# Time-step columns widened by a third of the z product, and the delta rule's diagonal blocks packed 64 wide

## What is computed

```
proj = x @ w_in                       # x 256x1024
z, xbc, dt_raw = proj[..., :1024], proj[..., 1024:2560], proj[..., 2560:2576]
xbc = silu(causal_dwconv(xbc, conv_w) + conv_b)
dt = softplus(dt_raw + dt_bias)       # 16 columns
da = dt * (-exp(a_log));  xdt = xs * dt
...                                   # chunk states, cumulative decays, y
y = y * silu(z)
```

## Time and profile before

| | us |
|---|---|
| median of 3 runs | 1343.62 |
| lowest, highest | 1341.12, 1346.0 |
| the profiled execution | 1346.43 |
| its span, first to last instruction | 1344.5 |
| PE busy in the span | 1290.2 |
| POOL busy | 947.8 |
| ACT busy | 648.8 |
| DVE busy | 416.1 |

### The profile page before, as it was taken

How to read it: one execution, slowest core, us unless ns; L and a number is a source line. 1 busy time by engine, 2 the same in 40 slices (tenths; PEclk the granted TensorE clock), 3 DMA queues, 4 the chain that set the end, 5 groups by cost and what they waited for, 6 DMA issues and landing times.

```text
span 1344.5 us, 19614 instructions
## 1 busy us (share of the span) xinstructions
PE 1290.2 (96%) x8203; PEld 1154.0 (86%) x8203; DVE 416.1 (31%) x755; ACT 648.8 (48%) x841; POOL 947.8 (70%) x416
## 2 busy tenths in 40 slices
PE   6999999999999999999999999999988878999997
PEld 6988988878899988897899889998878658999885
DVE  5526325442222210045552131101153452101124
ACT  5673545755455553343444454435356544443442
POOL 6864246846969888756478778879976346786983
PEclk9999999999999999998999999999999998999999
DMA  8744134534656555635355756646637334663651
GB/s 276 210 128 126 48 110 132 182 108 127 220 152 199 183 195 195 188 93 159 104 173 188 245 169 183 175 138 211 224 113 265 108 94 129 172 193 119 234 189 47
DMA packets 117966, 218.60 MB, mean 163 GB/s; under 512 B 9415, under 2 KB 18934, under 8 KB 117750
## 3 DMA queue, kind: packets, MB, share of 16 engines
q1 hardware_dynamic: 113888, 209.92, 50.6%
q10 hardware_dynamic: 3990, 7.42, 1.6%
HBM read 216.27 MB, written 1.05 MB: 162 GB/s over the span
## 4 chain that ended last, share of the span: by engine, by line
PE 89%; DVE 7%; ACT 2%; issue 1%; DMA 1%; ACTq 0%; DVEq 0%
PE acc L1868 13%; PE acc L1870 13%; PE acc L1871 13%; PE acc L1861 12%; PE acc L1863 12%; PE acc L1862 12%; PE pm L1876 8%; PE acc L1819 1%; PE acc L1820 1%; PE acc L1821 1%; ACT pm L548 1%; PE pm L1785 1%; DMA ct<-in_consts 1%; DVE XTlo L1063 0%; DVE pm L1734 0%
## 5 line engine op out<-in xcount | busy, mean ns | idle before, releaser
L533 POOL TENSOR_TENSOR wlo<-raw,whi 128x1024 fp32r<-128x1024 f32 (+2 forms) x412 | 947.6, 2325 | 382.1 <-ACT whi L548 380.6
L548 ACT ACTIVATE whi<-raw 128x1024 fp32r<-128x1024 f32 (+2 forms) x412 | 412.4, 1019 | 354.1 <-PE acc L1871 154.2
L1868 PE MATMUL acc<-XThi,whi 128*128 128x256 f32 x1424 | 406.8, 286 | 5.5 <-issue 2.9
L1870 PE MATMUL acc<-XTlo,whi 128*128 128x256 f32 x1424 | 405.3, 285 | 0.0
L1871 PE MATMUL acc<-XThi,wlo 128*128 128x256 f32 x1424 | 405.3, 285 | 0.0
L1868 PEld LDWEIGHTS acc<-XThi,whi 128*128 128x128 f32 x1424 | 275.8, 194 | 6.9 <-issue 3.7
L1870 PEld LDWEIGHTS acc<-XTlo,whi 128*128 128x128 f32 x1424 | 275.8, 194 | 0.2
L1871 PEld LDWEIGHTS acc<-XThi,wlo 128*128 128x128 f32 x1424 | 275.7, 194 | 0.0
L1861 PE MATMUL acc<-whi,XThi 128*128 128x512 f32 (+3 forms) x320 | 125.8, 393 | 2.6 <-DVE xbcT L1492 1.6
L1863 PE MATMUL acc<-whi,XTlo 128*128 128x512 f32 (+3 forms) x320 | 121.5, 380 | 0.0
L1862 PE MATMUL acc<-wlo,XThi 128*128 128x512 f32 (+3 forms) x320 | 121.5, 380 | 0.0
(11 more groups left out here) (405 smaller groups left out, 1657.7 us busy)
## 6 DMA issues: line engine op xcount, KB each, us to landing
raw<-in_w_in SPq DMA_DIRECT2D x68, 512.0 KB, 3.7
raw<-in_w_ff SPq DMA_DIRECT2D x64, 512.0 KB, 3.7
raw<-in_w_in_mix SPq DMA_DIRECT2D x44, 512.0 KB, 3.6
raw<-in_w_down SPq DMA_DIRECT2D x44, 512.0 KB, 4.3
raw<-in_w_gate SPq DMA_DIRECT2D x40, 512.0 KB, 3.6
raw<-in_w_up SPq DMA_DIRECT2D x40, 512.0 KB, 3.7
raw<-in_w_branch SPq DMA_DIRECT2D x16, 512.0 KB, 3.5
raw<-in_w_out_mix SPq DMA_DIRECT2D x16, 512.0 KB, 3.5
```

The source lines that it names most:

```text
L533: nc.gpsimd.tensor_tensor(wlo[:, u % SPLIT, 0:nk, 0:width], raw[:, u % RAW, 0:nk, 0:width], whi[:, u % SPLIT, 0:nk, 0:width].bitcast(F32), ...
L548: return nc.scalar.activation(out_, in_, func, **k)
L1868: T.matmul(o, wh[:, fs], hi[:, k, :], start=opens and f % 2 == 0, stop=False, skip_group_check=True)
L1870: T.matmul(o, wh[:, fs], lo[:, k, :], start=False, stop=False, skip_group_check=True)
```

## The change

Part A. The 16 columns of dt get the first 336 columns of z beside them, as one chunk "dt" of 352 columns; `pieces` loads them as two transfers. The rest of z is two chunks of 344. The chunk dt moves ahead of xbc2, and the small steps move with it: xs is transposed after one unit of xbc2, the C B step after one unit of mz1, sc0 gives its first unit to cover `rows(2)`, and DVE does dt's softplus before the convolution of xbc2. The z columns of chunk dt stay in `acc` until ACT has taken them, after the softplus, whose scratch lies in the free columns of the same bank.

Part B. The two 64x64 matrices of a tile lie one above the other: matrix j on partitions 64j to 64j+63, all eight tiles side by side in 512 columns in place of 1024. Each 128x128x128 matmul becomes two, one for each j: 64x64 with 64 moving columns on rows and columns 64j of the array for the levels and for the first transposition (now a product with the identity). For keys with keys and queries it is 128 rows by 64 columns; for u 64x64 with 128 moving columns; for w 64 rows by 128 columns with 64 moving columns. ACT's copies and DVE's masks and subtractions of these steps get half as many columns. The step that makes `d_e` is 16 operations on 64 partitions in place of 8 on 128.

```diff
 def pieces(c0, width):
...
+    if width == SSD_H + ZA:
+        return (c0, SSD_H), (0, ZA)
...
     for c in range(3):
+        if c == 2:
+            g.append(("dt", "w_in_mix", KD, M_DT, SSD_H + ZA, "T"))
         g.append((f"xbc{c}", "w_in_mix", KD, M_XBC + c * W, W, "F"))
-    g.append(("dt", "w_in_mix", KD, M_DT, SSD_H, "T"))
     for c in range(2):
-        g.append((f"mz{c}", "w_in_mix", KD, c * W, W, "T"))
+        g.append((f"mz{c}", "w_in_mix", KD, ZA + c * ZB, ZB, "T"))
...
-            high_halves(begun("mz0", 2) + AHEAD)
+            high_halves(begun("xbc2", 2) + AHEAD)
+            act.wait_ge(S["dt_done"], 1)
+            fn(zz[:, :, 0:ZA], accT("dt")[:, :, SSD_H:], ACT.Silu).then_inc(evac_at("dt")[0], 1)
+            high_halves(landed("xbc2") + AHEAD)
+            silu2(2)
+            leave("mz0", zz[:, :, ZA:ZA + ZB], ACT.Silu)
+            logs()
+            high_halves(begun("mz1", 1) + AHEAD)
             act.wait_ge(S["s_bt"], 1)
...
-                    mm(flat(i), kT[:, i:i + P], kT[:, i:i + P])
-                    last = mm(flat(2 * BANK + i), kT[:, i:i + P], qT[:, i:i + P])
+                    for j in range(2):
+                        at, cols = i // 2, slice(i + 64 * j, i + 64 * j + 64)
+                        mm(pm[diag(j), 0, at:at + 64], kT[:, cols], kT[:, cols])
+                        last = mm(pm[diag(j), 1, at:at + 64], kT[:, cols], qT[:, cols])
...
+            def blocks(hf, bank, lhs, rhs):
+
+                for k in range(4):
+                    for j in range(2):
+                        at = slice(hf * TOK + 64 * k, hf * TOK + 64 * k + 64)
+                        moving = ident[diag(j), diag(j)] if rhs is None else rhs[diag(j), at]
+                        last = mm(pm[diag(j), 2 * hf + bank, 64 * k:64 * k + 64], lhs[diag(j), at], moving)
+                return last
...
-                        if s < 5:
-
-                            mm(pm[:, 2 * hf + 1, j * P:(j + 1) * P], d_y[:, i:i + P], d_t1[:, i:i + P])
-                        last = mm(pm[:, 2 * hf, j * P:(j + 1) * P], d_t1[:, i:i + P], d_y[:, i:i + P])
-                    last.then_inc(S["dn_pq"], 1)
+                    if s < 5:
+                        blocks(hf, 1, d_y, d_t1)
+                    blocks(hf, 0, d_t1, d_y).then_inc(S["dn_pq"], 1)
...
-            product("xbc2", XThi, XTlo, 3, 4)
-            product("dt", XThi, XTlo)
-            from_x("mz0", 0, 2)
+            product("xbc2", XThi, XTlo, 1, 4)
+            from_x("mz0")
+            from_x("mz1", 0, 1)
             pe.wait_ge(S["s_xd"], 2)
```

More of the change, by code:

```diff
@@ L495, in build, with diag, own, by_tile @@
                   begun("ao1b", 0), begun("ao0c", 0), begun("ao0c", 1)]
+        def diag(j):
+            return slice(64 * j, 64 * j + 64)
+        def own(first, j):
+            return pm[diag(j), first:first + 2, :].rearrange("p a (k s) -> p (a k) s", s=P)[:, :, diag(j)]
+        def by_tile(ap):
+            return ap.rearrange("p (k s) -> p k s", s=64)
         def level_end(s):
@@ L673, in _ @@
             act.wait_ge(S["dn_qkn"], 1)
-            fn(d_br, pm[:, 2:4, :].rearrange("p a b -> p (a b)"), ACT.Copy)
+            for j in range(2):
+                fn(by_tile(d_br[diag(j)]), own(2, j), ACT.Copy)
             act.wait_ge(S["dn_e0"], 1)
@@ L863, in silu2 @@
                 fn(xbcT[:, 4 * j:4 * j + 4, :], xbcT[:, 4 * j:4 * j + 4, :], ACT.Silu).then_inc(S["silu2"], 1)
[L864 to L869, removed]
+            silu2(0)
+            turn("p0", PThi)
+            high_halves(landed("xbc1") + AHEAD)
+            silu2(1)
+            high_halves(landed("dt") + AHEAD)
             logs()
@@ L891, in _ @@
                 if hb == 1:
-                    leave("mz0", zz[:, :, 0:W], ACT.Silu)
-                    leave("mz1", zz[:, :, W:D], ACT.Silu)
+                    leave("mz1", zz[:, :, ZA + ZB:D], ACT.Silu)
                     logs()
@@ L1213, in _ @@
                 for t in range(NT):
[L1214 to L1217, removed]
+                    i = h * NT + t
+                    for j in range(2):
+                        last = V.tensor_scalar(d_e[diag(j), 64 * i:64 * i + 64], own(0, j)[:, i, :],
+                                               gcs[diag(j), t, h:h + 1], 0.0, ALU.subtract, ALU.min)
             last.then_inc(S["dn_e0"], 1)
@@ L1223, in _ @@
             v.wait_ge(S["dn_e"], 1)
[L1224 to L1227, removed]
+            for i in range(2):
+                last = V.scalar_tensor_tensor(out=pm[:, i, :], in0=d_e, scalar=1.0, in1=pm[:, i, :],
+                                              op0=ALU.min, op1=ALU.mult)
+            last.then_inc(S["dn_lt"], 1)
             v.wait_ge(S["dn_lt"], 1)
             v.wait_ge(S["dn_egr"], 1)
[L1230 to L1233, removed]
+            V.tensor_tensor(d_lt, pm[:, 0, :], d_br, ALU.mult)
+            V.tensor_tensor(by_tile(d_at), by_tile(pm[:, 1, :]), con("tri64c").unsqueeze(1).to_broadcast([P, 8, 64]),
+                            ALU.mult).then_inc(S["dn_lt"], 1)
             v.wait_ge(S["dn_kv"], 1)
@@ L1589, in finished @@
                 link(V.tensor_tensor(pm[:, 2, :], pm[:, 2, :], y, ALU.add))
[L1590 removed]
+                v.wait_ge(*evac_at("dt"))
+                for c in range(2):
+                    v.wait_ge(*evac_at(f"mz{c}"))
                 V.tensor_tensor(y, pm[:, 2, :], zz[:, b // 2, (b % 2) * W:(b % 2 + 1) * W], ALU.mult)\
@@ L2200, in _ @@
             turn("p0", pin)
-            product("xbc2", XThi, XTlo, 0, 3)
+            product("dt", XThi, XTlo)
+            product("xbc2", XThi, XTlo, 0, 1)
             pe.wait_ge(S["silu2"], 2)
@@ L2224, in _ @@
             mm(pm[:, 2, 2 * SSD_H:3 * SSD_H], ones, da[:, 0, :]).then_inc(S["s_ac"], 1)
-            from_x("mz0", 2, 4)
+            from_x("mz1", 1, 3)
             pe.wait_ge(S["s_btc"], 1)
@@ L2260, in heads_out @@
                 last.then_inc(S["b_y"], 1)
-            from_x("mz1", 1, 2)
             rows(0)
             rows(1)
-            from_x("mz1", 2, 4)
+            from_x("sc0", 0, 1)
             rows(2)
```

106 lines of the change are left out of this document (56 added, 50 removed).

## The result

| | before | changed |
|---|---|---|
| median, us | 1344.71 | 1330.22 |
| lowest, highest, us | 1341.12, 1346.0 | 1328.11, 1331.98 |
| profiled execution, us | 1346.43 | 1331.18 |
| its span, us | 1344.5 | 1329.4 |

The changed kernel takes 0.9891 of the time before, with a 95% interval of 0.9868 to 0.9913: 14.5 us less. The forecast was 9.4 us less, so the time lies 4 us under the predicted one and within its range.

The account below looks back on a forecast made before the run. PE, busy for 96% of the span, was taken to bound the kernel. Part A -7.0 (-4.3 - 2.5 - 2.4 + 2.2) and part B -2.4 made -9.4 us: 1343.6 to 1334.2 us, 8-in-10 range 1323 to 1346.

Parts of the forecast that it names:

- the price of a 64x64 pass: Delta rule: each pass of two 64x64 tiles in turn was taken at 0.045 us, for 608 passes.
- Part A, the widths: SSD mixer, matmuls of dt and mz: 0.162 us at 352 columns, 0.159 at 344; 27.3 to 23.0 us, -4.3 us.
- Part A, the waits that go: SSD mixer: PE's waits of 1.57 us ahead of mz0 and 0.96 us for POOL go, -2.5 us.
- Part A, the clock at dt: SSD mixer: the low clock after dt's 16-column matmuls and the idle time goes, -2.4 us.
- Part A, the wait that comes: SSD mixer, chunk state: PE waits for `xe`, held up by `eac` late on ACT, +2.2 us.
- rival 4: Part A gives less: the `xe` wait lowers the clock, another 2.5 us, or halves reach mz0 late; total -6.5, 1337; chance 0.15.
- X: The end of xbc2 on PE, from which the forecast counted its times in part A.
- Part B: Delta rule: 33.3 us go and 30.9 us come with the 64x64 tiles, -2.4 us.
- the low end: Delta rule: lowest bound for a pass, 0.026 us, from 64 moving columns alone and two tiles at a time.
- Rival 1: Delta rule: pairs don't overlap or issue sets the price, 0.057 to 0.062 us a pass; B +6.4, time 1343; chance 0.15.
- Rival 2: Delta rule: a 64x64 pass costs 0.105 us whatever moves, pairs don't help; B +33, about 1370; chance 0.07.
- Rival 3: Delta rule levels: the clock falls with a quarter of the array working; total +3 to +8, about 1349; chance 0.08.

Follow-up runs that it names:

- eac_early: The changed kernel with `bmt` and `eac` put ahead of the Silu of mz0 on ACT; 1328.54 us, ratio 0.9868 to the kernel before.
- narrow: The changed kernel with dt 16 columns wide again in its new place and z in two chunks of 512; 1335.86 us, ratio 0.9925 to the kernel before.
- hst_first: The changed kernel with `bmt` and `eac` earlier on ACT and the Silu of mz0 moved behind the copy `hst`; 1325.35 us, ratio 0.9857 to before.
- a_only: The kernel before with part A alone, the delta rule unchanged; 1340.17 us, ratio 0.995, 5.7 us less.
- b_only: The kernel before with part B alone, dt and z unchanged; 1334.57 us, ratio 0.9916, 11.3 us less.
- half_columns: The changed kernel with 32 moving columns in place of 64 in the levels and first transposition, only time counting; 1327.48 us.
- half_both: The changed kernel with 32 moving columns and 32 weight columns a pass in the levels and first transposition, only time counting; 1324.64 us.
- one_tile: The changed kernel with all products of the levels and first transposition on one quarter of the array; 1342.94 us, one execution.
- two_banks: The changed kernel with matrix 1's products in the levels and first transposition written to the pair's other bank, only time counting; 1329.05 us.
- after_again: The changed kernel measured again, without any edit; 1329.62 us, ratio 0.9884 to the kernel before.
- outer: The changed kernel with four tiles of one array quarter done before the four of the other in `blocks`; 1335.94 us, one execution.

## Why the prediction was right, and where it was not

In the sum the forecast was right: less by 9.4 us predicted, by 14.5 measured, inside its range. Its shares were the wrong way round. It expected most of the gain from A, and most came from B; the one term that was mis-sized is the price of a 64x64 pass, 0.045 us taken and 0.030 measured.

**Part A, the widths: right.** 0.162 us a matmul of dt was predicted and is 7.76 / 48 = 0.162. For 344 columns, 0.159 predicted: the 60 matmuls of mz0 and of mz1's first unit take 614.24 - 604.75 = 9.49 us in eac_early, 0.158.

**Part A, the waits that go: right.** No wait of PE is left ahead of mz0 or in it. ACT had the z columns of dt out at 604.3, half a microsecond before xbc2 ended at 604.76 on PE; it was worked out as level with it. Two errors nearly cancel there: DVE had the softplus done 1.2 us before, not 2, and the table load (at 598.70) was made before that, while ACT waited for DVE.

**Part A, the clock at dt: right.** Narrow matmuls and idle time were named together; narrow shows the fall under 16-column matmuls without idle time. It costs 2.0 us there; before, 2.4 were worked out.

**Part A, the wait that comes: right, and to the tenth by luck.** With X = 604.76, PE arrived at X + 15.15 (15.1 predicted) and went on at X + 17.3 (17.3 predicted); 2.2 us predicted, 2.17 measured. The count was made from ACT's order, element by element, and the order is what the experiments confirm. But `eac` came at X + 14.4, not 15.0, and `xe` took 2.72 us, not 2.28. In hst_first it took 1.23; the rest is a stand behind POOL (last section), and with `xe` at 1.23 some 1.5 of the 2.2 us would not have come. What the forecast left to rival 4 happened: the clock fell behind this wait. It cost 1.55 us and not 2.5. So A is -5.5 by the terms, -6.0 by a_only's stretch and -5.9 by the changed kernel's, and rival 4's mechanism is the truth for A, at a smaller price.

**Part B: the sign was right, the size wrong by 8 us, in one term.** That term is the price of a pass. Taken was 0.045; it is 0.030 between changes of tile size, and 0.033 with one (3.18 / 96). By steps, from start to start: keys 2.06, transposition 1.08, four levels of 3.18, the last 2.25, u and w 3.82, in all 21.9 us where 30.9 was predicted; before it was 33.3. That makes -11.3, of which the large units between give back some 0.6 (2.94 us in place of 2.85 each, six of them, and less in the others). The -10.7 left fits b_only: from the keys to `pin` it takes 583.39 - 95.69 = 487.7 us, before 594.42 - 95.90 = 498.5. The error was "not much below, since a pass is a weight load and a matmul and no row shows a long run of passes closer than 0.08": a lack of rows was taken as a sign of a cost. And the low end, 0.026, came from moving columns; half_columns and half_both show that it is the weight load that sets the end. That 0.026 lies near 0.030 is luck: both have 64 columns. The rows before held the price: a pass with 128x128 weights costs 0.111 whether 128 or 16 columns move, which is a price for 128 weight columns. Half of it for 64 columns and half again for two tiles in turn is 0.028. The step of u and w fits too: its u half is 32 passes of 128 moving columns in 1.72, and its w half, with 128 weight columns a tile, has 1.86 / 32 = 0.058, twice the levels' price. That step lost 0.3 us, 3.82 against 3.49.

The page "TensorE: Matmul & The Clock Gate" of the Trainium skill, section "LDWEIGHTS (loading the stationary operand)", says that a load takes the number of its columns divided by 1.2, in nanoseconds, whatever its rows. As an estimate from that figure, 128 columns take 0.107 us and 64 take 0.053. The traces agree to about a tenth: 0.111 a pass before, 0.059 in one_tile.

**Rival 1** (no overlap) is wrong: one_tile shows what its levels would have looked like, 0.059 a pass where the rival had 0.057 to 0.062. That its 1342.94 us is the rival's 1343 proves nothing: keys, u and w still overlap in it, and B costs 2 us there where the rival had 6.4. The rule that was weighed with it, "TensorEngine Tiling (Array Packing)" of the Trainium skill, section "Gotcha 1: PSUM Pressure", isn't what these runs show: the changed kernel's pairs write one bank on different partitions, and two_banks, which parts them, is no faster. Row tiles that write the same partitions of a bank were not tried. **Rival 2** (0.105 a pass) fell with it. **Rival 3** (the clock falls in the levels) didn't come; the granted clock was 1.00 over whole levels, in half_columns and one_tile too; what a longer run of such passes without full units between would do, no run shows.

**The rest.** The changed kernel's profiled execution was 17.1 us ahead at the first head group and 15.1 at its end; after_again's had 17.2 at its end (1344.5 - 1327.3). So what one of them gives back later differs from one execution to the next and need not be a part of the change. The dip of the scan is of that kind too: it is there in after_again (0.74 at 170 to 175) and not in the first profile of the same kernel. From the keys to `pin` the one takes 487.75 us, the other 486.32.

## What to carry to other kernels

Price a small matmul as two things, the columns of its weight load (here 0.111 us for 128, 0.059 for 64) and the columns that move (0.41 ns each and 0.018 us), and take the larger; then ask what runs beside it. Diagonal 64x64 blocks as two row-and-column tiles in turn bring a pass to about a quarter of a 128x128 one (0.030 against 0.111 us), if the instructions alternate tile by tile. And a matmul of 16 columns costs what its weight load costs (0.111 us) and can take the clock with it, so narrow columns belong beside wide ones; where such a move brings a new wait, count the waiting engine's queue by element, and change its order before accepting the wait.

## What the runs showed that was not expected

- The clock fell under a PE that was busy at every moment, with 128x128 weights and 16 moving columns (1.00 until 588.1, then 0.50), and didn't fall under passes of 64x64 tiles with 64 columns in turn, or under 32 moving columns (half_columns). These stood in stretches of 3.2 us with full units between.
- A load of 64x64 weights costs 0.030 us in turn with the other diagonal tile, 0.059 in one tile, and 0.042 with four of one tile ahead of four of the other, all with the same instructions. The column tiles of the keys' step (128 rows by 64 columns) overlap as well: 64 passes in 2.06 us, 0.032 each with the change of tile size.
- `xe` on DVE, the same instruction on the same data, took 2.72 us in the changed kernel, 1.23 in hst_first and 2.28 before. POOL's rows beside it show what makes the difference. Timeline of DVE and POOL in the changed kernel, then in hst_first:

```profile
619.21 2.72 DVE L1556 TENSOR_TENSOR xe<-xdt,eac 128x1024 f32<-128x1024 f32 x1 [2.75 <-ACT eac L568]
618.48 2.38 POOL L553 TENSOR_TENSOR wlo<-raw,whi 128x1024 fp32r<-128x1024 f32 x1
620.81 3.32 POOL L553 TENSOR_TENSOR wlo<-raw,whi 128x1024 fp32r<-128x1024 f32 x1
```

```profile
617.25 1.23 DVE L1557 TENSOR_TENSOR xe<-xdt,eac 128x1024 f32<-128x1024 f32 x1 [0.30 <-ACT eac L568]
617.32 2.69 POOL L553 TENSOR_TENSOR wlo<-raw,whi 128x688 fp32r<-128x688 f32 x1
```

  `xe` ends 1.12 us after POOL's next low half starts in the one and 1.16 in the other, and that low half takes some 1.0 us longer than others of its size (2.38 and 1.65). In before, b_only, a_only, narrow, eac_early, after_again, two_banks, half_both, one_tile and outer `xe` ends 1.1 to 1.2 us behind such a start as well. So `xe` stands until the low half that POOL is at has ended, and then POOL's next one stands for `xe`: its time depends on how far POOL is when `eac` comes. No run moved POOL alone; this is read from the rows.
